# A 31-tap depthwise convolution moved whole onto VectorE, its taps taking two channel groups in turn

## The reference

```
def _even_mix(h, w_in, a_conv_w, a_conv_b, a_ln_g, a_ln_b, a_pw_w, a_pw_b, b_fw, w_out):
    a_val, a_glu, a_gate, b_val, b_gate = _split(h @ w_in, [A_WIDTH, A_WIDTH, A_WIDTH, B_WIDTH, B_WIDTH])
    u = a_val * jax.nn.sigmoid(a_glu)
    u = jax.nn.silu(_layernorm(_dwconv(u, a_conv_w) + a_conv_b, a_ln_g, a_ln_b))
    y_a = (u @ a_pw_w + a_pw_b) * jax.nn.silu(a_gate)
    y_b = _fourier_mix(b_val, b_fw) * jax.nn.silu(b_gate)
    return jnp.concatenate([y_a, y_b], axis=-1) @ w_out
```

## Time and profile before

| | us |
|---|---|
| median of 3 runs | 918.42 |
| lowest and highest | 917.73, 918.75 |
| span of the profiled execution, first to last instruction | 915.92 |
| VectorE busy | 694.6 |
| TensorE busy | 821.0 |
| GpSimd busy | 159.5 |
| ScalarE busy | 462.4 |

### The profile page before, as it was taken

How to read it: one execution, slowest core, us unless ns; L and a number is a source line. 1 busy time by engine, 2 the same in 40 slices (tenths; PEclk the granted TensorE clock), 3 DMA queues, 4 the chain that set the end, 5 groups by cost and what they waited for, 6 DMA issues and landing times.

```text
span 915.9 us, 13840 instructions
## 1 busy us (share of the span) xinstructions
PE 821.0 (90%) x5384; PEld 733.0 (80%) x5384; DVE 694.6 (76%) x924; ACT 462.4 (50%) x635; POOL 159.5 (17%) x109
## 2 busy tenths in 40 slices
PE   0599999998898999999978997699699989999976
PEld 0499988877797999999977886588478788888875
DVE  4975488877866999999984999999669383946552
ACT  2444368767435555455455556644551561444451
POOL 0000023221000311321220069855300000000000
PEclk9799999999998999999997999799989999999988
DMA  9986696755533556657661221121206322722101
GB/s 353 376 288 264 253 323 237 247 211 200 208 139 138 210 210 268 238 220 264 246 223 47 105 126 46 47 92 58 81 20 258 109 83 102 291 78 93 47 1 47
DMA packets 26043, 156.73 MB, mean 171 GB/s; under 512 B 2659, under 2 KB 7052, under 8 KB 7820
## 3 DMA queue, kind: packets, MB, share of 16 engines
q1 hardware_dynamic: 21360, 148.91, 44.0%
q10 hardware_dynamic: 4636, 7.18, 2.5%
HBM read 155.01 MB, written 1.06 MB: 170 GB/s over the span
## 4 chain that ended last, share of the span: by engine, by line
PE 55%; DVE 26%; issue 10%; ACT 5%; DVEq 1%; ACTq 1%; DMA 1%; POOL 0%; POOLq 0%
PE wide L1133 21%; PE bank L1133 19%; DVE w_lo L753 9%; DVE arena L993 5%; DVE w_lo L783 4%; DVE arena L919 2%; PE bank L1478 2%; PE wide L1500 2%; PE bank L1361 2%; ACT w_hi L363 1%; DVE att L814 1%; DMA raw<-in_w 1%; PE bank L1491 1%; PE wide L1221 1%; PE bank L1480 1%
## 5 line engine op out<-in xcount | busy, mean ns | idle before, releaser
L783 DVE TENSOR_TENSOR w_lo<-raw,w_hi 128x2048 fp32r<-128x2048 f32 x93 | 218.8, 2354 | 50.3 <-ACT w_hi L363 48.0
L1133 PE MATMUL bank<-h_hi,w_hi 128*128 128x256 f32 x736 | 214.6, 292 | 22.6 <-DVE h_lo L819 13.2
L1133 PE MATMUL bank<-h_lo,w_hi 128*128 128x256 f32 x736 | 212.0, 288 | 0.0
L1133 PE MATMUL bank<-h_hi,w_lo 128*128 128x256 f32 x736 | 211.7, 288 | 0.0
L1133 PE MATMUL wide<-h_hi,w_hi 128*128 128x256 f32 (+1 forms) x528 | 182.2, 345 | 30.4 <-DVE w_lo L783 13.5
L363 ACT CAST w_hi<-raw 128x2048 fp32r<-128x2048 f32 x93 | 177.1, 1905 | 47.9 <-PE bank L1133 19.9
L1133 PE MATMUL wide<-h_lo,w_hi 128*128 128x256 f32 (+1 forms) x528 | 177.2, 336 | 0.0
L1133 PE MATMUL wide<-h_hi,w_lo 128*128 128x256 f32 (+1 forms) x528 | 176.9, 335 | 0.0
L1133 PEld LDWEIGHTS bank<-h_hi,w_hi 128*128 128x128 f32 x736 | 144.8, 197 | 24.6 <-issue 19.1
L1133 PEld LDWEIGHTS bank<-h_lo,w_hi 128*128 128x128 f32 x736 | 145.2, 197 | 0.0
L1133 PEld LDWEIGHTS bank<-h_hi,w_lo 128*128 128x128 f32 x736 | 145.1, 197 | 0.0
(11 more groups left out here) (239 smaller groups left out, 1149.2 us busy)
## 6 DMA issues: line engine op xcount, KB each, us to landing
raw<-in_w SPq DMA_DIRECT2D x141, 1024.0 KB, 4.8
xs<-in_xs ACTq DMA_DIRECT2D x2, 1024.0 KB, 12.7
consts<-diff ACTq DMA_DIRECT2D x8, 128.0 KB, 6.2
cond<-in_cond ACTq DMA_DIRECT2D x1, 1024.0 KB, 6.3
out<-xs SPq DMA_DIRECT2D x2, 512.0 KB, 3.0
consts<-in_c ACTq DMA_DIRECT2D x1, 576.0 KB, 3.9
arena<-in_cond ACTq DMA_DIRECT2D x1, 512.0 KB, 7.3
consts<-in_c ACTq DMA_DIRECT2D x1, 512.0 KB, 3.4
```

What stands on the lines that cost most here:

```text
L783: nc.vector.tensor_tensor(w_lo[:, slot, :], raw[:, rslot, :], w_hi[:, slot, :].bitcast(F32), ALU.subtract).then_inc(sem("lo_done"), 1)
L1133: last = mm(out, w[a], x[b], start=start and n == 0, stop=stop and n == 2, skip_group_check=skip)
```

## The change

All 31 taps of all four groups are made by VectorE. Groups 0 and 1 come first and take turns, tap by tap, and then groups 2 and 3; an instruction waits for the last but one before it, which is the one that wrote the same accumulator. All taps have 512 columns. 124 instructions replace 93, and 76 of them stand in steps 2 to 8 of the loop, 11 in a step (10 in step 4), and 48 in step 9. The waits for `glu_done` and `pads_set` stand ahead of each tap. ScalarE's products and GpSimd's additions go, with their buffers and semaphores; ScalarE gets one wait for `glu_done` at i = 6, since `glu` and `sgate` share their place. TensorE sums the groups in the order 0, 1, 2, 3, each as soon as its own last tap is made.

```diff
-CONV_VECTOR = {2: [(0, 0, 13)], 3: [(0, 13, 25)], 4: [(0, 25, 31), (2, 0, 4)], 5: [(2, 4, 16)], 6: [(2, 16, 28)],
-               7: [(2, 28, 31), (3, 0, 14)], 8: [(3, 14, 31)]}
-CONV_SCALAR = {2: [(1, 0, 7)], 3: [(1, 7, 14)], 4: [(1, 14, 21)], 5: [(1, 21, 28)], 6: [(1, 28, 31), (3, 0, 6)],
-               7: [(3, 6, 17)], 8: [(3, 17, 28)], 9: [(3, 28, 31)]}
-PRODS = 3
+CONV_TAPS = [(t + d, k) for t in (0, 2) for k in range(CONV_W) for d in range(2)]
+CONV_AFTER = {2: (0, 11), 3: (11, 22), 4: (22, 32), 5: (32, 43), 6: (43, 54), 7: (54, 65), 8: (65, 76), 9: (76, 124)}
...
@@ gpsimd
-            n = 0
-            for t in (1, 3):
-                pool.wait_ge(sem("conv_opened"), 1 if t == 1 else 2)
-                for k in range(1, CONV_W):
...
-                    nc.gpsimd.tensor_tensor(acc, acc, prod, ALU.add).then_inc(sem("prod_used"), 1)
-                    n += 1
@@ scalar
-                for t, k0, k1 in CONV_SCALAR.get(i, ()):
...
+                    if i == 6:
+                        act.wait_ge(sem("glu_done"), 2)
@@ vector
-                for t, k0, k1 in CONV_VECTOR.get(i, ()):
-                    dve.wait_ge(sem("glu_done"), 1 if t == 0 else 2)
+                for n in range(*CONV_AFTER.get(i, (0, 0))):
+                    t, k = CONV_TAPS[n]
+                    dve.wait_ge(sem("glu_done"), 1 if t < 2 else 2)
                     dve.wait_ge(sem("pads_set"), 2)
...
+                    acc, src = conv_part(t, k)
+                    if k == 0:
+                        ins = nc.vector.tensor_scalar(acc, src, col("a_conv_w", t), col("a_conv_b", t), ALU.mult, ALU.add)
+                    else:
+                        dve.wait_ge(sem("conv_tap"), n - 1)
+                        ins = nc.vector.scalar_tensor_tensor(acc, src, col("a_conv_w", 4 * k + t), acc, ALU.mult, ALU.add)
+                    ins.then_inc(sem("conv_tap"), 1)
@@ tensor
-            for n, t in enumerate((0, 2, 1, 3)):
-                if t != 1:
-                    pe.wait_ge(sem("conv_tap"), CONV_W * {0: 1, 2: 2, 3: 3}[t])
-                if t in (1, 3):
-                    pe.wait_ge(sem("prod_used"), (CONV_W - 1) * (1 if t == 1 else 2))
-                last = mm(bank[2][:, :], ones, conv[:, t, :], start=(n == 0), stop=(n == 3))
+            for t in range(4):
+                pe.wait_ge(sem("conv_tap"), 2 * CONV_W * (t // 2 + 1) + t % 2 - 1)
+                last = mm(bank[2][:, :], ones, conv[:, t, :], start=(t == 0), stop=(t == 3))
```

More of the change, by code:

```diff
@@ L185, in build @@
         four = [att[:, 0:512], att[:, 512:1024]]
-        conv_prod = [att[:, 1024 + 512 * n:1536 + 512 * n] for n in range(PRODS)]
         q_raw = arena[:, 0:1024]
@@ L210, in shift_col, with conv_part @@
             return modc(base + k // 2, k % 2, v)
[L212 to L218, removed]
+        def conv_part(t, k):
+            return conv[:, t, :].rearrange("p (s n) -> p s n", s=2), u_pad[:, t, :, k:k + T]
         def mod_row(base, v):
@@ L592, in fourier_out @@
                 nc.scalar.copy(y_b[:, g, :], bank[1][:, :]).then_inc(sem("y_b_raw"), 1)
-            n_prod = 0
             for i in range(10):
                 split(LIN_EIN + i + 2)
-                for t, k0, k1 in CONV_SCALAR.get(i, ()):
[L598 to L612, removed]
                 act.wait_ge(sem("lin_done"), LIN_OPEN + LIN_EIN + i + 1)
@@ L968, in _ @@
             norm("even_ctx", 5)
-            taps = 0
             for i in range(10):
```

## The result

| | before | changed |
|---|---|---|
| median, us | 918.08 (4 runs, 917.32 to 918.75) | 921.75 (4 runs, 921.09 to 922.36) |
| ratio to before, 95% interval | | 1.0044 (1.0030 to 1.0058) |
| span of the profiled execution, us | 915.92 | 920.6 |
| VectorE busy, us | 694.6 | 678.1 |
| GpSimd busy, us | 159.5 | 92.0 |

The changed kernel is 3.7 us slower, with 16.5 us less work on VectorE and 67.5 us less on GpSimd. In an experiment the numbers behind its edit are a few higher.

What follows compares the result with a forecast made beforehand. VectorE's slow taps bound the kernel up to 594.70, then TensorE up to the group sums. Last tap +2.7, group sums -0.2 and squares +0.8 gave +3.3 on 918.42: 921.7 us, range 917.4 to 925.4.

Steps and rivals of the forecast that it cites:

- Steps 2 to 8 are TensorE's: In steps 2 to 8, VectorE's 11 taps and remainder take less than TensorE's 10.90 us; chunk 8 ends at 607.1.
- 48 taps start 93.0 after chunk 1's end: Step 9's taps start at 616.9, behind ScalarE's rounding (7.6 after chunk 8) and the remainder (2.20).
- A tap costs 0.665: Alternating 512-column taps on VectorE overlap and follow 0.665 us apart; 48 take 32.0.
- Rival (a): VectorE's taps don't overlap (the drain rule), each costs 0.78: 5.5 us more, 927.2; chance 0.10.
- GpSimd's four instructions cost 4.0: GpSimd's four multiplications all fall into the last 48 taps and cost VectorE 1.0 us each, 4.0 together.
- Rival (b): GpSimd's four multiplications cost VectorE nothing, since queued taps hold the reads: -4.0, 917.7, no change; chance 0.13.
- Last tap 2.7 later: VectorE's last tap ends at 652.9 against 650.20 before, 2.7 us later.
- Group sums -0.2: TensorE's group sums are ready 2.9 after the last tap, at 655.8; order and clock together give -0.2 us.
- Squares +0.8: TensorE's sum of squares, partly at low clock after the idle, costs 0.8 us more; bounds 0 and 3.3.
- Nothing downstream: Behind the squares nothing else hangs on the taps; the product starts at low clock in both kernels.
- Rival (c): Faster: TensorE's end stays at full clock and GpSimd's multiplications cost VectorE nothing: 915.3; chance 0.07.

Runs made afterwards that it cites:

- the better table: Changed kernel with 11, 12, 11, 12, 14, 20, 20 taps in steps 2 to 8 and 24 in step 9: 900.09 us, ratio 0.9807.
- the scratch work: Changed kernel with 40 more 512-column multiplications on GpSimd from glu_done on, in buffers nobody reads: 927.26 us in one run.

## Why the prediction was right, step by step

Forecast 921.7, measured 921.75; that the last digit agrees is luck. Two terms missed by about 1 us each in opposite directions, and the forecast stands on the 918.42 of the profile's runs: the change was forecast as +3.3 and is +3.7 to the 918.08 measured beside it.

- *Steps 2 to 8 are TensorE's.* Chunk 8 was to end 183.2 us after chunk 1, and did after 183.1 (608.08 - 525.00). `w_lo` is waited for no more. Right.
- *48 taps start 93.0 after chunk 1's end.* 92.9 (617.94). VectorE idles 6.5 ahead of them. Right; the kernel with the remainder behind the taps shows what that start costs, 8.7 us.
- *A tap costs 0.665.* 0.662, by the alternation of L819 and L814 alone. The Trainium skill's rule that I quoted against the overlap, in "VectorE: DVE Perf Modes", section "The DRAIN you can't avoid", isn't what these taps show: with an unmet wait 0.787, without 0.662. The same section adds that a next instruction that isn't held starts earlier; I had left that out. Rival (a) was priced with 0.78; with the three waits as the change writes them it would have been 0.884 and 931.6.
- *GpSimd's four instructions cost 4.0.* The size was right, the reason was half right. I took each to come in at once. The first came in 15 us later, at a certain place in VectorE's stream, and where it isn't let in there the cost is nothing. Rival (b), at 0.13, was this: the kernels with the remainder behind the taps, with the fewer waits and with the better table show it, and so does the one with the scratch work, with streams that keep GpSimd out for 10 to 27 us. The rows gave me only cases in which GpSimd was in already, or the taps waited for each other.
- *Last tap 2.7 later.* 2.5.
- *Group sums -0.2.* +0.1: they came 3.2 after the last tap in place of 2.9.
- *Squares +0.8.* +1.7. I let the clock rise about 5 us after TensorE resumed, as in the earlier trace rows. It rose 8.8 us after (653.2 to 662), TensorE having paused for 1.4 us between. This term was mis-sized; with TensorE kept busy, or with the last taps 5.4 us later, it is 0.
- *Nothing downstream.* -0.8. The 512x512 product took 13.43 us in place of 13.88, since less of it fell under the low clock; the other 0.4 I haven't placed.
- *Rival (c).* Its mechanism is real: full clock and no contention are worth 3.5 and 4.0 us, each shown alone. It didn't occur, as the idle of TensorE said.

## What to carry to other kernels

Making an engine's work cheaper doesn't help where its last batch is tied to a late event: ask of the work that is left what releases it, and put it into the idle time ahead of earlier waits. Here the table of the taps was worth 22 us, and the removal of 60 contended additions without it lost 4. Let a chain of dependent Vector instructions alternate between two accumulators (0.125 us a tap here). Take redundant waits out of the inner loop: here two of them cost every tap one more instruction, and made an unmet wait 0.10 us dearer. And where TensorE is left idle ahead of work that the end waits for, count the low clock behind the idle into the price, 3.5 us here.

## What the hardware showed that I had not expected

- A run of queued taps can keep a GpSimd instruction out to its end: GpSimd's first multiplication lasted 9.7, 19.0, 25.6 and 26.6 us in four kernels, and 11.0 and 15.0 in those where it got in inside the run. Once GpSimd is in and has the next one ready, the two take turns, and each pair costs 1.45 to 1.67 us where the tap alone costs 0.66.
- VectorE's stream has a place, moved by instructions put ahead of it and marked by a load of instructions, where such a run let GpSimd in: 0.36 us more of idle time where taps wait for each other, nothing to be seen where they don't but GpSimd's entry. In two kernels of five GpSimd was waiting there and didn't get in.
- A wait that isn't met yet costs 0.10 us more in an instruction of its own than on the instruction that it holds (0.884 against 0.787).
- When TensorE resumed after the idle, the clock came back 8.8 us later in the changed kernel, 5.7 after the idle of 6.97 us before. The length of the idle doesn't settle it: after 23 us of idle it came back 3.6 us later (each tap waits, two waits hoisted), after 13.8 us 9.2 later (GpSimd behind the taps), after 5.0 us 4.4 later (remainder behind the taps).
